# A four-branch mixer trunk on one core: one product drained earlier in the search, a rows unit loaded in halves, and mixer D's tiles solved four at a time

## The chip, the cores and the metric

One core of one Trainium2 chip runs the whole program, in float32. The metric is the device time of one execution in microseconds; the median of three runs is compared.

## The reference, cut to what matters

Two layers run one after the other on x (1024 positions, 1024 channels). Each normalises x, multiplies it by one wide matrix `w_in`, and splits the result into inputs of four mixers, their gates and four merge gates:

```python
for l in range(DEPTH):                                   # 2
    h = _rmsnorm(x, norm_g[l]); p = h @ w_in[l]          # 1024 x 8904
    oa = _chunk_band_attention(aq, ak, av, bias) * silu(az)
    ob = _hgrn2(bq, bf, bi, ...) * silu(bz)              # gated linear recurrence
    oc = _dsa(...) * silu(cz)   # index scores, top 256 keys of each row, attention over them
    od = _rwkv7(dr, dk, dv, wd, ad, ...) * silu(dz)
    y = sum(sigmoid(g_b) * (o_b @ w_branch[l, b]) for b in 'ABCD')
    x = x + y @ w_out[l]
return _rmsnorm(x, final_g)
```

D (`_rwkv7`) is a recurrence over positions with a 64x64 state per head, four heads:

```python
def step(state, xs):
    rt, wt, kt, vt, kkt, at = xs
    sa = einsum('bhvk,bhk->bhv', state, -kkt)
    state = state * wt[:, :, None, :] + sa[..., None] * (kkt * at)[:, :, None, :] + vt[..., None] * kt[:, :, None, :]
    return state, einsum('bhvk,bhk->bhv', state, rt)
```

Its decays and rates come from small products: `tanh(wd) @ w_up` and `ad @ a_up`, each over 64 inner rows.

## The kernel before

Positions stand in eight tiles of 128 (`NT`). The mixers run in the order C, D, B, A; TensorE (`pe`), ScalarE (`act`), VectorE (`dve`), GpSimd (`pool`) and SyncE (`sp`, which issues the loads) each have their own program, written in order, and meet at semaphores.

**Fills.** The projection `h @ w_in` is not a stage of its own. It is cut into steps, and `pe_fill(pe, n)` puts n of them wherever TensorE would otherwise wait; the numbers are the table at the top of the file (`TOPK_FILL`, `D_FILL`, `B_FILL` and others). Blocks of 256 weight columns form units: a column unit has 7 products of four steps (the seven-product form of a 2x2 block product, `PRODUCTS`), and its sums of weight blocks (t1 to t4) and of results are made by GpSimd (`pool_w_sums`, `pool_fills`). A rows unit takes two blocks and computes four pairs of row tiles. Each product goes to one of two PSUM banks (`G`); ScalarE drains it (`act_product`, L528, L537, L541, L547), and `act_fills(act, key)` says up to which point in TensorE's order it drains before it goes on with its own work. Steps of a unit stand at L474 (512 columns) and L471 (256, two matmuls a step). All steps that are left at the end are done before the branch products, so their total does not depend on the tables. `FILL_ORDER` names the projections; gates fill in whenever a projection is not yet free (`next_unit`, `fill_after`).

**The search (C).** After the index scores VectorE looks for the 256th largest score of each row bit by bit, 32 bits (L1481 to L1490); two of the six row tiles are counted by ScalarE with a Sign (L1399). Beside it TensorE does `TOPK_FILL` steps. ScalarE drains between its counts by a formula:

```python
def beside(k, half):
    passed = 10 + (47 * k) // 10 + 2 * half + 7 * sum(k >= bit for bit in qk_bits) + 8 * (k >= 16)
    act_fills(act, ("beside search", min(passed, searched[0] - 1)))
act_fills(act, ("beside search", 12))
```

Then C's attention: scores (L1003), a row maximum on VectorE, Exp on ScalarE (L1083), transposes of the probabilities (L1014) drained by ScalarE (L1069), values (L1027).

**D.** First its products from the two low-rank codes (L1805, 64 rows in the array, eight matmuls through the banks T and O, each drained by a Tanh at L2003), which wait for the tanh of `wd` (L1997). Then norms, bonus and decays, transposes of v (L1831). Then pairs of tiles, four pairs: transposes of keys (L1869), products of keys and queries (L1848, `AG` and `CH`), the values of a chunk (L1856), and five levels that invert a triangular 64x64 system: per level Y (L1856, 16 matmuls of 64x64), masked by VectorE into `yy` (L2147), then X (L1904, 32 matmuls), subtracted by VectorE (L2150, L2151), then the next level. After it the solution (`UZ`), the transitions (`R`, `P`) and four steps of the state, each of which needs the state that VectorE copied (L2172). The table `D_FILL` puts one step after Y, two after X, three at most of the other places. `oD` is the bank of outputs that ScalarE drains (L2037).

**B** begins with its own preparation on VectorE and ScalarE beside `B_FILL["start"]` steps taken four times, then transposes (L1551).

**x.** At the start of layer 0 four DMAs load x, two tiles each (L2272); ScalarE squares and sums each tile (L880), VectorE normalises (L906), TensorE transposes (L413).

## Time and profile before

| what | us |
|---|---|
| median of three runs | 2880.6 (2878.49 to 2882.49) |
| the profiled execution | 2881.09 |
| its span, first to last instruction | 2879.3 |
| TensorE busy, matmuls | 2790.9 (97%), 18640 records |
| VectorE, ScalarE, GpSimd busy | 1584.4, 967.6, 819.7 |
| mean granted TensorE clock | 0.990 |

Times in rows are microseconds from the span's start unless marked ns; PE is TensorE, DVE VectorE, ACT ScalarE, POOL GpSimd. A float32 matmul leaves two records. "[0.59 <-ACT arena L2003]" is idle time of the engine just before a row and what ended it. Merged rows end with the last record's latency, about 0.2 us after the next can begin. PEclk is the granted share of 2.4 GHz: 1.00 is 2.4 GHz, 0.50 is 1.2 GHz. Layer 0 fills 0 to 1440 us, layer 1 the rest, in the same order.

### The profile page before, as it was taken

The page shows a single profiled execution, that of the slowest core. Times are in us where ns is not written, and L with a number is a line of the kernel's source. Part 1 is how long each engine was busy: PE and PEld are TensorE (multiplying, and loading weights), DVE is VectorE, ACT ScalarE, POOL GpSimd, SP SyncE. Part 2 cuts the span into 40 slices and gives each one's busy share as a digit, 9 for nine tenths or more (in the row PEclk, how much of TensorE's full clock was granted, in tenths as well). Part 3 has the DMA queues.
Part 4 walks back from the last instruction along what each step waited for, and adds up shares of the span by engine and source line. Part 5 has one row for each costly group of instructions (what it writes and reads, how often), then busy time and mean ns, then how long its engine had stood idle before and what let it go on. Part 6 is the DMA issues. An engine that isn't in the chain of part 4 may idle for free. (4 is left out here: it accounts for less than half of the span.)

```text
span 2879.3 us, 45819 instructions
## 1 busy us (share of the span) xinstructions
PE 2790.9 (97%) x18640; PEld 1493.9 (52%) x18640; DVE 1584.4 (55%) x2979; ACT 967.6 (34%) x1824; POOL 819.7 (28%) x578
## 2 busy tenths in 40 slices
PE   7999999999999999999999899999999999999998
PEld 4436444477644475444444364544776445654443
DVE  2788865633368813065227888656332787130743
ACT  3345764311143335300114457543111433352001
POOL 4323312321144232233052233123211443212330
PEclk9999999999999999999999999999999999999999
DMA  5212101111121221263042111011011212212731
GB/s 211 63 44 59 45 30 45 44 32 32 35 85 34 96 92 48 99 224 112 0 155 58 51 37 44 30 44 44 32 32 50 70 49 93 77 55 92 239 101 59
DMA packets 134985, 204.61 MB, mean 71 GB/s; under 512 B 8920, under 2 KB 88952, under 8 KB 134008
## 3 DMA queue, kind: packets, MB, share of 16 engines
q1 hardware_dynamic: 116184, 167.59, 18.5%
q10 hardware_dynamic: 18592, 34.09, 3.2%
q8 instruction: 149, 2.44, 0.4%
q14 instruction: 60, 0.49, 0.1%
HBM read 146.07 MB, written 48.78 MB: 68 GB/s over the span
## 5 line engine op out<-in xcount | busy, mean ns | idle before, releaser
L474 PE MATMUL ps<-hT,wr 128*128 128x512 f32 x1792 | 830.7, 601 | 3.6 <-ACT wr L528 2.0
L474 PEld LDWEIGHTS ps<-hT,wr 128*128 128x128 f32 x1792 | 326.7, 191 | 371.0 <-issue 354.7
L474 PE MATMUL ps<-sums,wr 128*128 128x512 f32 x896 | 431.3, 610 | 14.0 <-ACT arena L537 13.9
L634 POOL TENSOR_TENSOR gts<-gts,wr 128x512 f32<-128x512 f32 x96 | 138.0, 1437 | 572.0 <-ACT wr L528 349.4
L474 PEld LDWEIGHTS ps<-sums,wr 128*128 128x128 f32 x896 | 164.2, 194 | 192.8 <-issue 168.4
L1102 DVE CUSTOM_DVE_ANT_0 arena<-ps,arena 128x640 f32<-128x640 f32 (+7 forms) x128 | 90.4, 706 | 306.9 <-PE ps L1003 292.7
L713 PE MATMUL ps<-xo,arena 128*128 128x512 f32 x512 | 220.2, 592 | 1.6 <-ACT gts L541 1.6
L528 ACT ACTIVATE wr<-ps 128x512 f32<-128x512 f32 x168 | 99.6, 593 | 358.6 <-PE ps L474 315.4
L474 PE MATMUL ps<-wr 128*128 128x512 f32 x448 | 210.7, 599 | 1.3 <-ACT wr L528 1.3
L1485 DVE TENSOR_SCALAR_CACHE_REDUCE arena<-arena,sm 128x384 f32<-128x384 uint16 (+7 forms) x256 | 192.8, 809 | 2.2
L607 POOL TENSOR_TENSOR wr<-wr 128x512 f32<-128x512 f32 x62 | 84.7, 1365 | 363.6 <-PE ps L474 356.8
L1399 ACT ACTIVATE arena<-arena,sm 128x896 f32<-128x896 uint16 (+3 forms) x128 | 139.4, 1089 | 69.4 <-DVE sm L1481 69.1
L713 PEld LDWEIGHTS ps<-xo,arena 128*128 128x128 f32 x512 | 97.1, 190 | 124.7 <-issue 124.7
L880 ACT ACTIVATE arena<-arena 128x1024 f32<-128x1024 f32 x24 | 25.4, 1058 | 396.7 <-DVEq L959 392.3
L634 POOL TENSOR_TENSOR arena<-arena,wr 128x512 f32<-128x512 f32 x48 | 79.1, 1649 | 255.8 <-ACT wr L528 173.9
L537 ACT ACTIVATE arena<-ps 128x256 f32<-128x256 f32 (+1 forms) x144 | 68.4, 475 | 214.4 <-PE ps L474 101.7
L471 PE MATMUL ps<-wr,hT 128*128 128x256 f32 x576 | 139.1, 385 | 0.8 <-ACT arena L537 0.8
L1069 ACT ACTIVATE arena<-ps 128x512 f32<-128x512 f32 (+3 forms) x192 | 88.5, 461 | 140.3 <-PE ps L1014 138.7
L547 ACT ACTIVATE gts<-ps 128x512 f32<-128x512 f32 x96 | 57.0, 594 | 220.3 <-PE ps L474 203.4
L474 PEld LDWEIGHTS ps<-wr 128*128 128x128 f32 x448 | 81.1, 190 | 91.3 <-issue 85.8
L1458 DVE SCALAR_TENSOR_TENSOR arena<-arena,sm 128x512 f32<-128x512 f32 (+3 forms) x140 | 104.9, 749 | 28.9 <-ACT arena L1381 24.5
L471 PEld LDWEIGHTS ps<-wr,hT 128*128 128x128 f32 x576 | 106.3, 190 | 18.0 <-ACT arena L537 1.6
(308 smaller groups left out, 4366.8 us busy)
## 6 DMA issues: line engine op xcount, KB each, us to landing
wr<-in_w_in SPq DMA_DIRECT2D x68, 1024.0 KB, 5.3
gate_tanh<-gts ACTq DMA_DIRECT2D x128, 256.0 KB, 2.1
arena<-gate_tanh SPq DMA_DIRECT2D x128, 256.0 KB, 2.9
x_cur<-arena SPq DMA_DIRECT2D x2, 4096.0 KB, 23.0
arena<-in_w_branch SPq DMA_DIRECT2D x8, 1024.0 KB, 9.9
wr<-in_w_out SPq DMA_DIRECT2D x8, 1024.0 KB, 6.6
arena<-x_cur SPq DMA_DIRECT2D x4, 2048.0 KB, 8.8
arena<-arena SPq DMA_DIRECT2D x36, 128.0 KB, 2.8
```

The source lines that it names most:

```text
L471: ins = pe.matmul(ap[:, 0:NCB], lhsT=left(h_side, kt)[:, P * i:P * i + P], rhs=right(u, w_side)[:, kt, :], start=fresh and kt == 0, stop=k ...
L474: ins = pe.matmul(ap, lhsT=right(u, w_side)[:, kt, :], rhs=left(h_side, kt), start=fresh and kt == 0, stop=kt == half_k - 1, skip_group_ch ...
L528: jobs.emptied(act.activation(stage_of(u), src, ACT.Copy), key)
L537: jobs.emptied(act.activation(dest_of[key[:2]](i, slot), src, ACT.Copy), key)
L607: pool.tensor_tensor(t1[:, k0:], b12[:, k0:], b11[:, k0:], ALU.subtract).then_inc(sg("w_sums"), 1)
L634: pool.tensor_tensor(dst, dst, stage_of(u), ALU.add).then_inc(sg("pool_added"), 1)
L713: ins = pe.matmul(ap, lhsT=wbs[ORDER.index(b)][:, k2, P * ct:P * ct + P], rhs=xo[:, 2 * ORDER.index(b) + k2, 512 * half:512 * half + 512], ...
L1069: ins = act.activation(probs_t[u % 3][:, P * g:P * (g + n)], ap[:, 0:P * n], ACT.Copy)
L1102: ins = dve.tensor_tensor_reduce(out=rows[u % 2][:, 0:P * nb], in0=ap[:, 0:P * nb], in1=bias(i, h, nb), scale=HD ** -0.5, scalar=-3e38, op ...
L1399: act.activation(compared[i], half_keys(k // 16, i), ACT.Sign, bias=cand[:, j:j + 1], scale=-1.0, accum_out=count[:, j:j + 1]).then_inc(sg ...
L1458: ins = dve.scalar_tensor_tensor(acc, r, wgt, acc, ALU.mult, ALU.add)
L1485: ins = dve.tensor_scalar(compared[i], half_keys(part, i), cand[:, j:j + 1], None, ALU.is_lt, ALU.add, accum_out=count[:, j:j + 1])
```

## The change

- Search: `TOPK_FILL` 181 becomes 194; ScalarE drains up to step 16 before its first count, and by a new formula beside it. Steps of the key selection are divided differently over four units of attention.
- Rows unit: the second weight block is loaded in two halves (`fill_top_loaded`), the upper one a product earlier; GpSimd makes t1 from the first block and that half, and t2 after it.
- D's first products: `D_FILL["start"]` becomes 4 with 4 more behind a new mark, and ScalarE drains to the mark before the tanh.
- D's tiles by four: two pairs with buffers of their own, level by level in turn, one fill step in each level between Y and X of both; one step of the state of the first pair between solutions of the second. B's projections may begin only when D's outputs are drained, since their place now holds the second pair's buffers.
- Attention: the second transpose group is drained before finished fills, not behind them.
- x: eight loads of one tile.

```diff
-TOPK_FILL = 181
+TOPK_FILL = 194
-D_FILL = {"start": 6, "kk": 23, "bonus": 37, "decay": 11, "nat": 2, "AG": 3, "CH": 3, "Y": 1, "X": 2, "UZ": 3, "P": 3, "S": 1, "norm": 12, "turn": 24}
-B_FILL = {"start": 13, "end": (6, 6), "khn": (3, 2), "adds": (3, 3, 3, 13, 1), "att": 1, "last": 2, "turn": 8}
+D_FILL = {"start": 4, "kk": 23, "bonus": 37, "decay": 11, "nat": (2, 2), "CH": (5, 5), "Y": 1, "UZ": 2, "R": 1, "P": (2, 2), "S": (1, 1), "norm": 13, "turn": 24}
+B_FILL = {"start": 14, "end": (6, 6), "khn": (3, 2), "adds": (3, 3, 3, 13, 1), "att": 1, "last": 2, "turn": 8}
...
-            fill_after = {("B", 0): ("oT", "C", NT - 1), ("B", 3): ("oT", "C", NT - 1), ("B", 1): ("vn", NT - 1),
+            fill_after = {("B", 0): ("oD", NT // 2 - 1), ("B", 3): ("oD", NT // 2 - 1), ("B", 1): ("oD", NT // 2 - 1),
...
+                    if n in second:
+                        top_done = (*done[:3], 4)
+                        loads.append((top_done, wr[:, 2 + n % 2, 0:half_k, 0:w], c0, w, sg("fill_top_loaded"), sums_of, 0))
+                        loads.append((done, wr[:, 2 + n % 2, half_k:, 0:w], c0, w, sg(f"fill_w_loaded{n % 2}"), sums_of, half_k))
+                        continue
...
-                        ap = act_ready(act, ("PT", b, u, g))
+                        key = ("PT", b, u, g)
+                        ap = jobs.ready(act, key) if g else act_ready(act, key)
...
-                        passed = 10 + (47 * k) // 10 + 2 * half + 7 * sum(k >= bit for bit in qk_bits) + 8 * (k >= 16)
+                        passed = 18 + (426 * k) // 100 + 2 * half + sum(n for bit, n in ((4, 9), (12, 9), (16, 9), (23, 3), (27, 2)) if k >= bit)
-                    act_fills(act, ("beside search", 12))
+                    act_fills(act, ("beside search", 16))
...
                     pe_fill(pe, D_FILL["start"])
+                    jobs.mark("before Dw")
+                    pe_fill(pe, 4)
                     pe.wait_ge(sg("wd_tanh"), 1)
...
+                    act_fills(act, "before Dw")
                     act.wait_ge(sg("wd_shifted"), 1)
...
+                    for p in range(0, NT // 2, 2):
+                        turn_keys(p)
+                        pe_fill(pe, D_FILL["nat"][0])
+                        local_products(p)
+                        pe_fill(pe, D_FILL["CH"][0])
+                        turn_keys(p + 1)
+                        chunk_values(p)
+                        pe_fill(pe, D_FILL["nat"][1])
+                        local_products(p + 1)
+                        pe_fill(pe, D_FILL["CH"][1])
+                        chunk_values(p + 1)
+                        for lv in range(1, 6):
+                            for e in range(2):
+                                level_y(p + e, lv)
+                            pe_fill(pe, D_FILL["Y"])
+                            for e in range(2):
+                                level_x(p + e, lv)
+                        for j in range(2):
+                            solve(p, j)
+                        pe_fill(pe, D_FILL["UZ"])
+                        transitions(p)
+                        added_values(p)
+                        pe_fill(pe, D_FILL["P"][0])
+                        state_step(p, 0, 0)
+                        solve(p + 1, 0)
+                        state_step(p, 0, 1)
+                        solve(p + 1, 1)
+                        state_step(p, 1, 0)
+                        pe_fill(pe, D_FILL["S"][0])
+                        state_step(p, 1, 1)
+                        transitions(p + 1)
+                        pe_fill(pe, D_FILL["R"])
+                        added_values(p + 1)
+                        pe_fill(pe, D_FILL["P"][1])
+                        for n in range(4):
+                            if n:
+                                pe_fill(pe, D_FILL["S"][1])
+                            state_step(p + 1, n // 2, n % 2)
...
-                            sp.dma_start(xin[:, 2 * n:2 * n + 2, :], x_pairs[:, 2 * n:2 * n + 2, :]).then_inc(sg(f"x_in{n}"), 16)
+                        for i in range(NT):
+                            sp.dma_start(xin[:, i, :], x_tiles[:, i, :]).then_inc(sg(f"x_in{i}"), 16)
```

Three places of the order, in layer 0. The first is TensorE in D's levels (x counts matmuls, each of which leaves two records in the trace). Before, L1856 is Y and L1904 X, of one pair:

```order
L1856 MATMUL ps<-arena 64x64 x16
L474 MATMUL ps<-hT,wr 128x512
L1904 MATMUL ps<-arena 64x64 x32
L474 MATMUL ps<-hT,wr 128x512 x2
L1856 MATMUL ps<-arena 64x64 x16
L474 MATMUL ps<-hT,wr 128x512
L1904 MATMUL ps<-arena 64x64 x32
```

And in the changed program, where L1873 is Y and L1935 X, of both pairs:

```order
L1873 MATMUL ps<-arena 64x64 x32
L474 MATMUL ps<-hT,wr 128x512
L1935 MATMUL ps<-arena 64x64 x64
L1873 MATMUL ps<-arena 64x64 x32
L474 MATMUL ps<-sums,wr 128x512
L1935 MATMUL ps<-arena 64x64 x64
L1873 MATMUL ps<-arena 64x64 x32
```

The steps after X are gone, and X of the second pair is followed at once by Y of the first pair's next level. The second place is ScalarE at D's first products; before, the tanh of wd (L1997) comes first and the drains of fills behind it:

```order
L1995 ACTIVATE arena<-arena 128x2048
L1997 ACTIVATE arena<-arena 64x1024
L541 ACTIVATE gts<-ps 128x512
L559 ACTIVATE gts<-gts 128x512
L537 ACTIVATE arena<-ps 128x512
L559 ACTIVATE gts<-gts 128x512
L565 DMA gate_tanh<-gts 128x512 x2
L2003 ACTIVATE arena<-ps,sm 128x512 x8
```

Now (L2074 is that tanh, L2080 the drains of D's first products):

```order
L2071 ACTIVATE arena<-arena 128x2048
L547 ACTIVATE gts<-ps 128x512
L2074 ACTIVATE arena<-arena 64x1024
L528 ACTIVATE wr<-ps 128x512
L559 ACTIVATE gts<-gts 128x512
L2080 ACTIVATE arena<-ps,sm 128x512 x8
```

One drain and one tanh are left between the tanh of wd and the drains that TensorE waits for, instead of four operations and two stores. The third place is ScalarE at the search's start, before and now (L1399 and L1411 are the counts, L528 and L537 drains of fills):

```order
L528 ACTIVATE wr<-ps 128x512
L537 ACTIVATE arena<-ps 128x512
L1399 ACTIVATE arena,sm<-arena,sm 128x896
L1399 ACTIVATE arena,sm<-arena,sm 128x1024
L1399 ACTIVATE arena,sm<-arena,sm 128x896
L537 ACTIVATE arena<-ps 128x512
```

```order
L528 ACTIVATE wr<-ps 128x512
L537 ACTIVATE arena<-ps 128x512 x2
L1411 ACTIVATE arena,sm<-arena,sm 128x896
L528 ACTIVATE wr<-ps 128x512
L1411 ACTIVATE arena,sm<-arena,sm 128x1024
L1411 ACTIVATE arena,sm<-arena,sm 128x896
```

A second drain stands ahead of the first count, and the next one between the first two counts instead of behind the third.

## Rows read from the trace of the kernel before

**Rows 1.** The page, part 1: busy time, share, instructions of each engine.

```profile
PE 2790.9 (97%) x18640; PEld 1493.9 (52%) x18640; DVE 1584.4 (55%) x2979; ACT 967.6 (34%) x1824; POOL 819.7 (28%) x578
```

**Rows 2.** TensorE's waits: us in total, times, longest.

```profile
PE ps L474 <- ACT arena L537: 13.9, 2, 7.0
PE ps L413 <- DVE xo L906: 13.8, 1, 13.8
PE ps L1014 <- ACT arena L1069: 10.3, 17, 1.3
...
PE ps L1869 <- issue: 3.4, 6, 0.6
```

**Rows 3.** Timeline, the search's start: start, us, operation; layer 0, last row layer 1.

```profile
199.67 5.63 PE L474 MATMUL ps<-sums,wr 128*128 128x512 f32 x8 [6.97 <-ACT arena L537]
205.13 3.60 PE L474 MATMUL ps<-hT,wr 128*128 128x512 f32 x8
...
194.34 1.04 ACT L1399 ACTIVATE arena<-arena,sm 128x896 f32<-128x896 uint16 x1 [7.88 <-DVE sm L1481]
...
1631.06 6.72 PE L474 MATMUL ps<-sums,wr 128*128 128x512 f32 x8 [6.97 <-ACT arena L537]
```

**Rows 4.** Timeline of TensorE and GpSimd at C's rows unit, layer 0.

```profile
224.00 1.10 PE L471 MATMUL ps<-wr,sums 128*128 128x256 f32 x4 [1.52 <-POOL wr L606]
...
232.25 1.99 PE L471 MATMUL ps<-wr 128*128 128x256 f32 x8 [1.19 <-ACT rows_stage L528]
...
333.38 3.70 PE L474 MATMUL ps<-hT,wr 128*128 128x512 f32 x8 [1.01 <-ACT wr L528]
...
221.23 1.28 POOL L604 TENSOR_TENSOR wr<-wr 128x512 f32<-128x512 f32 x1 [3.10 <-DMA wr<-in_w_in]
```

**Rows 5.** TensorE in a stretch: length, busy (records), PEclk, DMA share, GB/s.

```profile
470.00:480.00 10.00, 10.00 (x13) 0.50 0.00 1
```

**Rows 6.** Timeline of TensorE at D's first products, layers 0 and 1.

```profile
467.22 1.98 PE L1805 MATMUL ps<-arena,par 64*128 64x512 f32 x4 [0.55 <-ACT arena L1997]
469.80 10.04 PE L1805 MATMUL ps<-arena,par 64*128 64x512 f32 x12 [0.59 <-ACT arena L2003]
479.76 5.52 PE L474 MATMUL ps<-hT,wr 128*128 128x512 f32 x8
...
1902.32 9.09 PE L1805 MATMUL ps<-arena,par 64*128 64x512 f32 x12 [0.59 <-ACT arena L2003]
1911.35 4.83 PE L474 MATMUL ps<-hT,wr 128*128 128x512 f32 x8
```

**Rows 7.** Timeline of VectorE as the tiles of x land.

```profile
11.43 0.15 DVE L893 TENSOR_SCALAR sm<-sm 128x1 f32<-128x1 f32 x1 [0.28 <-DMA arena<-in_x]
...
13.97 0.15 DVE L893 TENSOR_SCALAR sm<-sm 128x1 f32<-128x1 f32 x1 [0.28 <-DMA arena<-in_x]
```

**Rows 8.** Timeline of ScalarE in C's attention: a fill's drain.

```profile
407.29 0.58 ACT L528 ACTIVATE wr<-ps 128x512 f32<-128x512 f32 x1
```

**Rows 9.** Timeline of D's levels, layer 0, first pair: TensorE, then VectorE.

```profile
591.49 1.15 PE L1856 MATMUL ps<-arena 64*64 64x64 f32 x32
592.57 1.12 PE L474 MATMUL ps<-hT,wr 128*128 128x512 f32 x2
593.63 1.16 PE L1904 MATMUL ps<-arena 64*64 64x64 f32 x64
...
596.63 1.15 PE L1856 MATMUL ps<-arena 64*64 64x64 f32 x32
...
592.69 0.69 DVE L2147 TENSOR_TENSOR arena<-ps,con 128x512 f32<-128x512 f32 x1 [1.69 <-PE ps L1856]
594.85 0.69 DVE L2150 TENSOR_TENSOR arena<-arena,ps 128x512 f32<-128x512 f32 x1 [1.47 <-PE ps L1904]
595.46 0.68 DVE L2151 TENSOR_TENSOR arena<-arena,ps 128x512 f32<-128x512 f32 x1
```

**Rows 10.** Timeline of TensorE at B's first transposes, layer 0.

```profile
891.40 1.04 PE L1551 MATMUL ps<-con,arena 128*128 128x128 f32 x8
```

More of the change, by code:

```diff
@@ L505, in act_fills @@
                     after = fill_after.get(key[:2])
-                    if after is not None and after[1] == "D":
+                    if after is not None and after[0] == "oT" and after[1] == "D":
                         jobs.stored(act, after)
@@ L1858, in by_chunk, with tiles, turn_keys @@
                         return ins
-                    for p in range(NT // 2):
-                        tiles = ((0, 2 * p), (1, 2 * p + 1))
-                        for j, i in tiles:
+                    def tiles(p):
+                        return ((0, 2 * p), (1, 2 * p + 1))
+                    def turn_keys(p):
+                        e = p % 2
+                        for j, i in tiles(p):
                             t0, t1 = P * i, P * i + P
@@ L1879, in pe @@
-                        jobs.filled(ins, ("CH", p))
-                        pe_fill(pe, D_FILL["CH"])
-                        jobs.stored(pe, ("CH", p))
+                            last = products(ap, i, 0, ((bet, alp, True), (bet, rho, False), (bet, alp, False), (alp, bet, True)))
+                            jobs.filled(last[1], ("AG", i))
+                        for n, bk in enumerate((T, O)):
+                            jobs.open(pe, ("CH", p, n), bk)
+                        for j, i in tiles(p):
+                            last = products(both, i, 2 * j, ((kap, alp, False), (kap, rho, False)))
@@ L1882, in pe, with chunk_values @@
+                        for n in range(2):
+                            jobs.filled(last[n], ("CH", p, n))
+                    def chunk_values(p):
+                        e = p % 2
                         ap = jobs.open(pe, ("CV", p), O)
-                        for j, i in tiles:
-                            ins = by_chunk(ap, 256 * j, HD, ct_[:, j], vn[:, i, :].rearrange("p (h v) -> p h v", h=4))
+                        for j, i in tiles(p):
+                            ins = by_chunk(ap, 256 * j, HD, ct_[e][:, j], vn[:, i, :].rearrange("p (h v) -> p h v", h=4))
@@ new lines, in level_x @@
+                    def level_x(p, lv):
+                        e, key = p % 2, ("X", p, lv)
+                        jobs.stored(pe, ("Y", p, lv))
+                        ap = jobs.open(pe, key, S2[e])
+                        for j in range(2):
+                            for h in range(4):
+                                for crossed, x, y in ((True, xt[e][:, j], yy[e][:, j]), (False, yy[e][:, j], xt[e][:, j])):
+                                    if crossed and lv == 5:
+                                        continue
+                                    for c in range(2):
+                                        rows, c0 = half_rows(c, False), (0 if crossed else 512) + 256 * j + CH * h
+                                        ins = pe.matmul(ap[half_rows(c, crossed), c0:c0 + CH], lhsT=x[rows, h, :], rhs=y[rows, h, :],
+                                                        start=True, stop=True)
+                        jobs.filled(ins, key)
@@ new lines, in solve, with transitions @@
+                    def solve(p, j):
+                        e, i = p % 2, 2 * p + j
+                        pe.wait_ge(sg(f"x_ready{e}"), 6 * (p // 2) + 6)
+                        ap = jobs.open(pe, ("UZ", i), (T, O)[j])
+                        jobs.stored(pe, ("CV", p))
+                        jobs.stored(pe, ("nat", i))
+                        jobs.filled(by_chunk(ap, 0, P, xt[e][:, j], acv[e][:, j]), ("UZ", i))
+                    def transitions(p):
+                        e = p % 2
+                        for j, i in tiles(p):
@@ L1926, in pe, with added_values @@
                                         jobs.filled(ins, ("R", p, c))
+                    def added_values(p):
+                        e = p % 2
                         ap = jobs.open(pe, ("P", p), S2[1])
-                        for j, i in tiles:
+                        for j, i in tiles(p):
                             for h in range(4):
@@ L1952, in pe @@
                                     rows = slice(CH * c, CH * c + CH)
-                                    pe.matmul(o[rows, oc(j, h)], lhsT=gt_[rows, j, h, :], rhs=uz[rows, j, h, HD:], start=j == 0 and h < 2, stop=True,
+                                    pe.matmul(o[rows, oc(j, h)], lhsT=gt_[e][rows, j, h, :], rhs=uz[e][rows, j, h, HD:], start=j == 0 and h < 2, stop=True,
                                               skip_group_check=True)
@@ L2156, in dve, with take_transitions @@
+                        link(dve, ins)
+                        for n in range(2):
+                            jobs.emptied(dve.engine_nop(), ("CH", p, n))
+                        dve.wait_ge(sg(f"x_ready{e}"), 6 * (p // 2) + 1)
+                    def take_transitions(p):
+                        e = p % 2
                         for c in range(2):
```

305 lines of the change are left out of this document (152 added, 153 removed).

## The prediction

> **What bounds the kernel.** I read the busy times of the page first, then TensorE's waits, then the timeline at its longest ones, then the granted clock there. TensorE is busy 2790.9 us of 2879.3, every other engine 55% or less [rows 1]: its own work is the bound. That work is the same after the change: the same products, and 968 fill steps per layer in both programs (a fill step is one float32 128x512 matmul, or two of 128x256; the trace shows each matmul as two records, at 0.4285 us, so a step is 0.857 us). Moving a step costs nothing by itself. The change can only win what lies between: TensorE's idle time, 88.4 us in all, of which four named waits make 41.4 [rows 2]; stretches at the low clock; and the handovers between full-array fills and 64x64 products, which count as busy. What it can lose is new idle time.
>
> **The search.** In both layers TensorE stands 6.97 us, until ScalarE empties a bank. The reader is to see that ScalarE sat 7.88 us at the same time, waiting in order for VectorE's first candidate at 194.34, with a finished product undrained [rows 3]. Behind the gap the clock is granted at the low level, 1.2 GHz: the next eight records take 5.63 and 6.72 us where the same eight take 3.60 at 2.4 GHz. So the price is 2 x 6.97 + 2.03 + 3.12 = 19.1 us. The change drains one more product before that wait (16 steps instead of 12) and one between the first two counts. One product is 3.43 us of TensorE, from 192.6 to 196.0, and the second drain follows ScalarE's count at 194.34 + 1.04, at about 195.4. Gap and low clock both go: **-19.1**. The 13 added steps are 11.1 us of work brought forward, so TensorE reaches the attention when it did before, with VectorE's search ending there too.
>
> **Rows unit.** Here the weight sums come late on GpSimd: it waits 3.10 us for the second weight block, starts at 221.23, and each half sum takes 1.27 [rows 4]. TensorE waits 1.52, then 1.38 for the fourth sum, later 1.19 (stage buffer), 0.42 and 1.01 (drains behind schedule). The upper half of the block now loads one product (3.4 us) earlier and the two halves of t1 need only it, so GpSimd can start when the last product of the unit before ends, at 218.9. t2's first half is then ready about 222.8 against 222.5 wanted, its second 0.3 late; the 1.19 stays near 1.1. Of 4.5 us per layer 2.0 stay: **-5.0** for two layers. The new drain table (4.26 steps per bit, where a bit takes 3.65 us) should remove most of the 1.01 per layer and little else: **-1.3**. Against that, B's three units, which ran among D's products, now run in one piece between D and B (95 steps), so B's rows unit has nothing beside it that hides its first sums and its stage: by the same count 1.5 per layer, **+3.0**. B's own start has 62 steps of fill ahead of its first transpose instead of 58, and TensorE did not wait there [rows 10], so I cost it at nothing; each us by which its chain on VectorE and ScalarE grew past those 3.4 us would be paid in full, twice.
>
> **D's first products.** Two waits, 0.55 (the tanh, ScalarE L1997) and 0.59 (a drain that stands behind ScalarE's other fills), precede sixteen 64-row records [rows 6]. From then on the granted clock is 0.50 [rows 5], and twelve records take 10.04 and 9.09 us against 5.3 at the full clock; the next eight 5.52 and 4.83 against 3.60. Sum: 2.3 + 4.7 + 3.8 + 1.9 + 1.2 = 13.9 us. The change gives two more steps of cover (1.7 us, over the 0.55) and drains older fills before the tanh. What is left is one bank exchange per two matmuls: 0.69 drain plus latencies against the other matmul's 0.857, some 0.1 each, 0.7 in all. What preceded the fall was half-empty rows together with both gaps; with the gaps gone I expect 2.4 GHz to hold: **-13.2**. The low end is -14, the other -2 (clock falls anyway). By the Trainium skill (TensorE: Matmul & The Clock Gate, The HAM clock gate) the gate follows how busy the engine was, idle lowers it and sustained work releases it: by that rule records without gaps keep the high level, and the term would be the same. The trace agrees only in part: twelve 64-row records back to back did not raise it again.
>
> **Loads of x.** Pairs of tiles land 2.54 us apart and VectorE waits for each [rows 7], so a tile is worked off in less than half of that, 1.27, and the second of the last pair only behind the first. Single tiles land 1.27 apart, the last at the same time as now but with nothing ahead of it: VectorE's norm, and with it TensorE's start (the 13.8 in [rows 2]), comes 1.2 us earlier: **-1.2**. Bounds: -2.5 (a whole tile) and +1 (four more issues ahead of the parameters and weights).
>
> **C's attention.** A drain of a finished fill (0.58) stands ahead of the drain of the second transpose group that TensorE waits for [rows 8]; the change turns the two round. It hits perhaps a third of the 17 waits that make 10.3 us. The selection's four steps on VectorE are evened out as well: **-3.0** (0 to -8).
>
> **D's tiles.** In the old levels a period is 5.14 us [rows 9]: 3 steps (2.57), Y's 32 records 0.94, X's 64 records 0.94, so 0.69 goes to four changes of array shape, 0.35 per fill burst. Per two pairs the old program has 36 bursts, the new 17. Outside the levels it is 16 against 12: 4 x 0.35 = 1.4 saved. In the levels 20 bursts become 5, but VectorE now shows. With X0 starting at 0: X0's result reaches VectorE at 1.22, its two subtractions start 0.61 apart and end, with the link, at 2.58; Y0 starts at 2.65, where TensorE was free at 1.88. VectorE turns to X1 at 2.6, is done at 3.96; Y1 starts at 4.02, free at 3.59. Y1 0.94, step and burst 1.21: the next X0 at 6.17. Less its one step that is 5.3; the old two periods less their six steps are 5.14. So 0.17 lost for each of four levels, 0.85 won in the fifth (only one subtraction follows): about nothing, 0.2. Then half of the waits on the output bank at L1869 go (3.4 us in six, [rows 2]): 1.1 per layer, of which I count 0.7. Per layer 2 x (1.4 + 0.2) + 0.7 = 3.9, **-8** for both. Nothing in the old trace shows paired levels; bounds: all 19 bursts won without waits, -27; one more VectorE operation (0.69) exposed in each of the 20 paired levels on top, +6.
>
> New small waits, at the search's end above all: **+1.5**. **Sum:** -19.1 - 5.0 - 1.3 + 3.0 - 13.2 - 1.2 - 3.0 - 8 + 1.5 = -46.3, from the profiled execution's 2881.1 to 2834.8; the median of the runs shown is 0.5 below that execution. I say **2835 us**.
>
> **Rivals.**
> (1) The clock still falls at D's first products, since half the array's rows are empty there with or without gaps. For: the low level held through the twelve back-to-back records. Against: it fell right behind the gaps. 11.5 us are lost: 2846.
> (2) The paired levels wait more than worked out, or run at 1.2 GHz now and then: 0.5 to 1 us in each of 20, so 2845 to 2855. For: between X1 and the next step TensorE does 1.9 us of Y at half the array in some 3.2 us, thinner than anything in the old levels. Against: there the clock is 1.00 throughout, with fills on half the time.
> (3) Slower than before: the low clock through all paired levels. X0, X1, Y0, Y1 and the step double; VectorE's share is hidden under them, and a period is about 9.6 us instead of 6.2. Twenty make +68, total about 2903; it decides from 14 of the 20. Against: at the low clock TensorE would be busy nearly all of that period, and after each low stretch in the trace dense work brought 2.4 GHz back. By the Trainium skill (the same page, A second HAM failure mode: psum-queue depth-cycling) short idles between matmul groups make the gate swing between its levels, which speaks for this one and (2).
> (4) The earlier drains do not carry: VectorE's search ends later than TensorE's 194 steps, and TensorE waits for its first probabilities. ScalarE was held 6 us in the rows unit, and GpSimd's sums then hold it still: some 5 per layer, 2845.
> (5) The paired levels hide better than I think: 2824.
>
> **How the numbers follow.** Forecast 0.50 (own range 2826 to 2844); (1) 0.18, (2) 0.15, (3) 0.03, (4) 0.06, (5) 0.08. The range 2822 to 2856 takes in all but (3) and the tails of (2). No case but (3) comes near 2880; a measurement tells 0.2%, 5.8 us, from no change. Faster by more than that 0.94, within 0.03, slower 0.03.
>
> **What would show it.** No wait on L537 near 193 us and granted clock 1.00 there; L1821's sixteen records (the old L1805) in about 7 us at 1.00; waits on GpSimd's sums under 1 us; new waits of 0.8 and 0.4 on VectorE between X1 and Y1 in each level, and 17 bursts per two pairs; half a wait left at the transposes of keys; attention starting no later. Low clock in 575 to 800 us, or a wait over 2 us at the first probabilities, would prove me wrong.

## The result and the profile after

The changed kernel takes 2854.85 us (median of 4 runs, 2853.26 to 2858.69); the kernel before, beside it, 2881.55 (2878.49 to 2887.02). The ratio is 0.9914, 95% interval 0.9894 to 0.9935. The gain is 26.7 us where 46 was forecast: the sign is right, the size is not. The profiled execution, the slowest of the four, took 2858.69 us, 22.4 less than that of before; the readings below are of these two executions.

The page, part 1, of the changed kernel:

```profile
PE 2770.7 (97%) x18640; PEld 1499.8 (52%) x18640; DVE 1589.2 (56%) x2979; ACT 961.9 (34%) x1820; POOL 844.0 (30%) x578
```

TensorE's waits (us in total, times, longest):

```profile
PE ps L413 <- DVE xo L917: 12.6, 1, 12.6
PE ps L1873 <- DVEq L2276: 10.9, 29, 0.6
PE ps L471 <- POOL wr L608: 8.5, 4, 3.7
PE ps L1025 <- ACT arena L1081: 7.4, 16, 0.8
PE ps L474 <- ACT xo L537: 5.5, 3, 2.2
...
PE ps L471 <- ACT rows_stage L528: 4.2, 5, 1.2
```

Against [rows 1, 2], TensorE is busy 20.2 us less with the same 18640 records, and idle 2.2 us less (86.2 instead of 88.4). The wait of twice 6.97 is gone. In its place stand three groups that the old list did not have at this size: 10.9 us on VectorE in D's paired levels, 8.5 on GpSimd's sum at L608, 5.5 on ScalarE's drain at L537.

To see where the rest went I cut TensorE's timeline at the same operations in both traces and took 0.857 us off for each fill step between two cuts, since steps only move. C's search, for instance, runs from the first index product to the first score product, with 240 steps before and 253 now. The two cuts, before and after:

```profile
90.20 1.77 PE L1358 MATMUL ps<-arena 64*128 64x384 f32 x8
...
350.11 0.49 PE L1003 MATMUL ps<-arena 64*128 64x128 f32 x4
```

```profile
90.20 1.77 PE L1370 MATMUL ps<-arena 64*128 64x384 f32 x8
...
357.74 0.49 PE L1014 MATMUL ps<-arena 64*128 64x128 f32 x4
```

259.9 - 240 x 0.857 = 54.2 us before, 267.5 - 253 x 0.857 = 50.7 now. All stretches, in us against the kernel before (kk is D's product of head sums, vn below stands for the transposes of v ahead of D's first tile):

| stretch of TensorE | forecast, both layers | layer 0 | layer 1 |
|---|---|---|---|
| start to first index product (x) | -1.2 | 0.0 | -0.3 |
| C's search, rows unit, drain table | -25.4, +1.5 small waits | -3.5 | -5.3 |
| C's attention, to its last product | -3.0 | -0.8 | -0.8 |
| D's first products, the wait ahead of them included, to kk | -13.2 | -7.3 | -5.8 |
| kk to D's first tile | 0 | +2.6 | +1.0 |
| D's tiles | -8 | -3.4 | -1.8 |
| D's end to B's first transposes | +3.0 | +2.8 | +2.8 |
| B, A and the output | 0 | -2.5 | -0.1 |
| sum | -46.3 | -12.1 | -10.3 |

Most of the miss is one line: the search wins 8.8 us where 24 was forecast. The first score product stands at 357.74, 7.6 later than before, since the 13 steps brought forward are 11.1 us of work and only 3.5 were won; by the prediction's own sign the attention was to start no later. The -2.5 of layer 0 in the last line is B's attention, from its first transposes to those of its gated outputs: less its steps it takes 35.1 us before and 32.6 now, in layer 1 34.7 and 35.2. Nothing in the forecast orders it, and in b_shift below, which moves 13 steps and nothing else, it takes 33.5 and 32.6, so this part of the gain is luck. The first stall itself is gone. ScalarE at the search's start, changed kernel:

```profile
189.31 0.60 ACT L537 ACTIVATE arena<-ps 128x512 f32<-128x512 f32 x1 [2.84 <-PE ps L474]
194.34 1.04 ACT L1411 ACTIVATE arena<-arena,sm 128x896 f32<-128x896 uint16 x1 [4.43 <-DVE sm L1493]
...
195.38 0.57 ACT L528 ACTIVATE wr<-ps 128x512 f32<-128x512 f32 x1
```

These are the drains at the times forecast, and in 190 to 200 us TensorE is busy throughout at granted clock 1.00, where [rows 3] has the stall. What was won there was lost in two later places. TensorE in the rows unit and at the z gate, then GpSimd and VectorE in the rows unit, and the row of a stretch (length, busy time and records of PE, PEld, DVE, ACT, POOL, granted clock, DMA):

```profile
217.87 4.19 PE L471 MATMUL ps<-wr,sums 128*128 128x256 f32 x8 [3.75 <-POOL wr L608]
221.85 2.67 PE L471 MATMUL ps<-wr,hT 128*128 128x256 f32 x8
...
314.47 7.97 PE L474 MATMUL ps<-hT,wr 128*128 128x512 f32 x14 [2.16 <-ACT xo L537]
```

```profile
211.23 2.08 POOL L604 TENSOR_TENSOR wr<-wr 128x512 f32<-128x512 f32 x1
213.27 2.24 POOL L605 TENSOR_TENSOR wr<-wr 128x512 f32<-128x512 f32 x1
215.48 2.24 POOL L608 TENSOR_TENSOR wr<-wr 128x512 f32<-128x512 f32 x1
...
209.89 2.29 DVE L1449 TENSOR_TENSOR arena<-arena,xo 128x1024 f32<-128x1024 f32 x1
212.22 2.17 DVE L1450 TENSOR_TENSOR arena<-arena 128x1024 f32<-128x1024 f32 x1
214.32 2.28 DVE L1448 TENSOR_TENSOR arena<-arena,xo 128x1024 f32<-128x1024 f32 x1
```

```profile
213.00:220.00 7.00, 3.18 (x11) 1.83 (x9) 6.97 (x4) 0.38 (x1) 7.00 (x5) 0.76 0.00 1
```

GpSimd's sums take 2.1 to 2.2 us each, not 1.28 [rows 4], and VectorE's rotary products beside them 2.2 to 2.3, not 1.2. The third sum ends at 217.72 and TensorE goes on at 217.87. Behind its 3.75 us the clock falls to its low level, 1.2 GHz (0.76 on average in this stretch): eight records take 4.19 us. Without the first stall TensorE reaches the rows unit 8 us earlier (its first product starts at 210.5), on top of VectorE's rotary step of q, which stands at bit 4 of the search. Before, GpSimd started at 221.23, when that step was over.

### The profile page after: what moved, and what is told of

It reads as the page before. It is cut to its first block and busy times, and to the rows that moved or that the text cites. A ratio compares the mean times of both kernels' runs of the same rounds, so it can differ in the third digit from the quotient of the medians.

```text
span 2856.9 us, 45851 instructions
## 1 busy us (share of the span) xinstructions
PE 2770.7 (97%) x18640; PEld 1499.8 (52%) x18640; DVE 1589.2 (56%) x2979; ACT 961.9 (34%) x1820; POOL 844.0 (30%) x578
## 5 line engine op out<-in xcount | busy, mean ns | idle before, releaser
L637 POOL TENSOR_TENSOR gts<-gts,wr 128x512 f32<-128x512 f32 x96 | 159.7, 1663 | 688.4 <-ACT wr L528 422.1
L528 ACT ACTIVATE wr<-ps 128x512 f32<-128x512 f32 x168 | 99.6, 593 | 316.4 <-PE ps L474 272.3
L610 POOL TENSOR_TENSOR wr<-wr 128x512 f32<-128x512 f32 x56 | 79.4, 1417 | 326.9 <-PE ps L474 322.7
L1411 ACT ACTIVATE arena<-arena,sm 128x896 f32<-128x896 uint16 (+3 forms) x128 | 139.4, 1089 | 74.2 <-DVE sm L1493 74.0
L891 ACT ACTIVATE arena<-arena 128x1024 f32<-128x1024 f32 x24 | 25.4, 1059 | 395.5 <-DVEq L970 392.3
L537 ACT ACTIVATE arena<-ps 128x256 f32<-128x256 f32 (+1 forms) x144 | 68.5, 476 | 215.1 <-PE ps L474 123.6
L1081 ACT ACTIVATE arena<-ps 128x512 f32<-128x512 f32 (+3 forms) x192 | 88.4, 461 | 135.3 <-PE ps L1025 133.8
L637 POOL TENSOR_TENSOR arena<-arena,wr 128x512 f32<-128x512 f32 x48 | 67.9, 1415 | 218.2 <-ACT wr L528 126.5
L547 ACT ACTIVATE gts<-ps 128x512 f32<-128x512 f32 x96 | 57.0, 594 | 222.2 <-PE ps L474 218.9
L618 POOL TENSOR_TENSOR wr<-wr 128x512 f32<-128x512 f32 x56 | 87.8, 1568 | 118.7 <-PE ps L474 118.7
## 6 DMA issues: line engine op xcount, KB each, us to landing
x_cur<-arena SPq DMA_DIRECT2D x2, 4096.0 KB, 24.8
```

The costliest lines, as they stand in the source:

```text
L528: jobs.emptied(act.activation(stage_of(u), src, ACT.Copy), key)
L618: pool.tensor_tensor(t4, b21, t2, ALU.subtract).then_inc(sg("w_sums"), 1)
L637: pool.tensor_tensor(dst, dst, stage_of(u), ALU.add).then_inc(sg("pool_added"), 1)
L1081: ins = act.activation(probs_t[u % 3][:, P * g:P * (g + n)], ap[:, 0:P * n], ACT.Copy)
L1411: act.activation(compared[i], half_keys(k // 16, i), ACT.Sign, bias=cand[:, j:j + 1], scale=-1.0, accum_out=count[:, j:j + 1]).then_inc(sg ...
```

## The experiments

All ran against the kernel before, which had medians of 2881.3 to 2881.8 us. The a_ runs are edits of the changed kernel and are set against its 2854.85, the b_ runs edits of the kernel before. Line numbers in rows are each run's own: D's first products are L1805, L1807, L1819 or L1821. "Search" is the stretch of the table, in us of layers 0 and 1: before 54.2 and 55.4, changed 50.7 and 50.1.

**a_rope: VectorE's rotary steps later.**

```diff
-                qk_bits = {4: 0, 12: 1}
+                qk_bits = {9: 0, 14: 1}
-                        passed = 18 + (426 * k) // 100 + 2 * half + sum(n for bit, n in ((4, 9), (12, 9), (16, 9), (23, 3), (27, 2)) if k >= bit)
+                        passed = 18 + (426 * k) // 100 + 2 * half + sum(n for bit, n in ((9, 9), (14, 9), (16, 9), (23, 3), (27, 2)) if k >= bit)
```

> The changed kernel with VectorE's rotary step for q moved from the search's bit 4 to bit 9 and for k from 12 to 14 (the drain table moved with it). Theory A (GpSimd's weight sums of the rows unit now run at the same time as VectorE's rotary products and both are slowed): the sums near 211 us take 1.27 us each instead of 2.06 to 2.24, the three slowed rotary products 1.2 instead of 2.3, TensorE's wait of 3.75 us for the second half of t2 falls below 1 us in both layers and the low clock behind it goes; 6 to 7 us per layer, about 2842 us. Theory B (the sums are late because the weight block's half arrives late or because they start late): the wait stays at 3 us or more, time within 3 us of 2855. Theory C (the search's end on VectorE bounds): the wait goes but TensorE waits as much for the first probabilities, 2850 to 2855.

Measured 2849.27 (2847.84 to 2851.35), ratio 0.9892 (0.9877 to 0.9907); search 46.3 and 46.3. GpSimd and TensorE of this run:

```profile
214.26 1.27 POOL L604 TENSOR_TENSOR wr<-wr 128x512 f32<-128x512 f32 x1
...
216.72 1.27 POOL L608 TENSOR_TENSOR wr<-wr 128x512 f32<-128x512 f32 x1
...
218.13 2.27 PE L471 MATMUL ps<-wr,sums 128*128 128x256 f32 x8 [1.59 <-POOL wr L608]
```

Full-speed sums, full-speed rotary products (1.21 to 1.63), no low clock. The wait is 1.59 rather than under 1, because GpSimd now starts at 214.26, behind an addition. 8.2 us of the stretch come back, 5.6 in the medians, where 12 to 14 was expected; theory A by mechanism, its size too high.

**a_z: one more drain before the z gate.**

```diff
                         if k == Z_BIT:
+                            beside(k, 3)
                             act_z_gate(act)
```

> The changed kernel with one more finished product drained on ScalarE just before the z gate's tanh at bit 22. Theory A (the new drain table leaves a finished product undrained while ScalarE loads its table and does the tanh, 3.1 us): TensorE's waits of 2.16 us near 312 us and in the second layer go, with the low clock behind them, 3 to 4 us per layer, about 2848 us. Rival (ScalarE's drain waits for GpSimd's addition, not for its own order): the waits only move by a product, time within 2 us of 2855.

Measured 2856.24 (2849.06 to 2858.87), ratio 0.9912 (0.9893 to 0.9931): no gain that can be told; search 48.9 and 48.6. The rival is right in its outcome, though not in its reason: the drain waited for ScalarE's own order. The 2.16 is gone, and TensorE waits 2.11 us some 18 us later in both layers, where the changed kernel had 1.21 in layer 1 and nothing over 0.4 in layer 0:

```profile
332.81 2.41 PE L474 MATMUL ps<-sums,wr 128*128 128x512 f32 x5 [2.11 <-ACT xo L537]
```

There ScalarE stands 3.11 us, waiting for bit 27's candidate, while VectorE multiplies in the z gate, with a finished product undrained: the first stall's pattern a third time.

**a_rows_undone: the second block in one piece, sums in the old order.**

```diff
-                    if n in second:
+                    if False:
...
-                        pool.tensor_tensor(t1[:, 0:k0], b12[:, 0:k0], b11[:, 0:k0], ALU.subtract).then_inc(sg("w_half_sums"), 1)
-                        pool.tensor_tensor(t1[:, k0:], b12[:, k0:], b11[:, k0:], ALU.subtract).then_inc(sg("w_sums"), 1)
...
```

> The changed kernel with the rows unit's part undone: the second weight block loads in one piece and both halves of t1 and t2 come in the old order, after the whole block. Theory A (collision with the rotary products is the cost): the sums start near 221 us and take 1.27 us each, the rotary products 1.2; TensorE waits about 1.5 and 1.4 us there instead of 3.75 and 0.53 and the clock stays high; 3 to 5 us per layer gained, about 2847 us. Rival (my forecast for this part: it wins 2.5 us per layer): undoing it costs 5 us, about 2860.

Measured 2861.56 (2858.24 to 2864.88), ratio 0.9934 (0.9918 to 0.995): 6.7 slower than the changed kernel. My expectation was wrong. The sums do not go back to 221 us: they start at 212.61, 1.4 later than with the change, and still meet the rotary step (2.03 to 2.24 us each). TensorE waits 2.80 and 3.22. What sets the moment is when TensorE arrives, not the order of the sums. The size is near the forecast's 5, but most of it comes from another place: C's search is only 0.7 and 1.6 us longer than in the changed kernel (51.5 and 51.7), while the stretch from D's end to B's first transposes is 2.2 longer in both layers. There, in B's rows unit, no rotary step is near, and TensorE waits for two sums instead of 0.48:

```profile
819.39 1.10 PE L471 MATMUL ps<-wr,sums 128*128 128x256 f32 x4 [1.39 <-POOL wr L606]
821.86 1.13 PE L471 MATMUL ps<-wr,sums 128*128 128x256 f32 x4 [1.37 <-POOL wr L611]
```

So this run does not show that the split wins 2.5 us in C's unit of the changed kernel; in B's unit it wins 2.2.

**a_dw_undone: D's first products as before.** In D_FILL "start" is 6 and "kk" 25, and:

```diff
-                    jobs.mark("before Dw")
-                    pe_fill(pe, 4)
-                    act_fills(act, "before Dw")
```

> The changed kernel with the part on D's first products undone: 6 steps ahead of them instead of 4 and 4, no earlier drain (two steps go back behind them). Theory A: two waits of about 0.55 us return, the clock falls to 0.50 in the products and stays there for 20 records, both layers lose what they won, 5 to 6.6 us each: 2865 to 2868 us. Rival (the steps of fill around them or luck set the clock there, not the gaps): the clock stays 1.00 and only about 1 us per layer returns, 2857.

Measured 2858.8 (2856.85 to 2861.5), ratio 0.9926 (0.9908 to 0.9943). The clock stayed at 1.00 and only one wait of 1.07 per layer came back, ahead of a fill. This is 4.0 slower than the changed kernel, near the rival's number; my theory of this part was in doubt, and the next two runs are for it.

```profile
473.48 1.12 PE L474 MATMUL ps<-sums,wr 128*128 128x512 f32 x2 [1.07 <-ACT gts L547]
474.54 7.68 PE L1819 MATMUL ps<-arena,par 64*128 64x512 f32 x16
```

**b_dw: that part alone on the kernel before.** The same edit the other way, with "kk": 21.

> The kernel before with the part on D's first products alone: 4 steps, a mark, 4 steps, and ScalarE drains up to the mark ahead of its tanh (two steps fewer behind). Theory A (the two waits beside the half-empty rows bring the low clock; without them it stays): the sixteen records take 7.7 us in one piece at granted clock 1.00, 5 to 6.6 us per layer gained, about 2869 us. Rival (what decides is at which fills of the unit the products fall, which the search's 13 steps moved, not this part; the run with this part undone kept the high clock): the clock falls to 0.50 here too, 2878 to 2882 us.

Measured 2869.57 (2865.41 to 2872.75), ratio 0.9962 (0.9949 to 0.9975): 11.9 less. The timeline of TensorE, against [rows 6]:

```profile
467.87 7.68 PE L1807 MATMUL ps<-arena,par 64*128 64x512 f32 x16
475.49 1.98 PE L474 MATMUL ps<-hT,wr 128*128 128x512 f32 x4
```

**b_shift: only the place.** The kernel before with `"start": 19` for `"start": 6`, nothing else.

> The kernel before with nothing but 13 more steps of fill ahead of D's first products (19 instead of 6, no mark and no earlier drain), so that these stand at the fill they have in the changed kernel, 13 steps on. The part alone on the kernel before won 12 us, and yet undoing it in the changed kernel cost only its 1 us wait per layer. Theory A (in the changed kernel the products fell at another place in ScalarE's row of fills, where the second wait does not come between the fourth and the fifth record; the place alone keeps the clock): one wait of about 1 us ahead of the sixteen records, these in about 7.7 us at granted clock 1.00, 5 us per layer gained, 2870 to 2872. Rival (the place does not matter and only the extra drain keeps the clock): two waits and 0.50 again, 2879 to 2883.

Measured 2871.16 (2869.47 to 2873.02), ratio 0.9971 (0.996 to 0.9982). One wait of 1.02 ahead of a fill, then sixteen records in 7.68 us at 1.00. So the edit alone keeps the clock, and so does moving the products by 13 steps. Both take away the 0.59 between the fourth and fifth record. The fall comes only with waits on both sides of four half-empty records: in both layers of the kernel before [rows 6], and again in both layers of b_rope7 below (0.55 and 0.59, then twelve records in 9.09 us). No run has one of the two waits without the other at this place, so which of them it takes stays open. The expected 12 us are real, but the search's 13 steps would have brought them anyway.

**a_search_undone: 181 steps, the old drain table.** The 13 steps stand ahead of D's first products ("start" 17).

```diff
-TOPK_FILL = 194
+TOPK_FILL = 181
-                        passed = 18 + (426 * k) // 100 + 2 * half + sum(n for bit, n in ((4, 9), (12, 9), (16, 9), (23, 3), (27, 2)) if k >= bit)
+                        passed = 10 + (47 * k) // 10 + 2 * half + 7 * sum(k >= bit for bit in qk_bits) + 8 * (k >= 16)
-                    act_fills(act, ("beside search", 16))
+                    act_fills(act, ("beside search", 12))
```

> The changed kernel with the search's part undone (181 steps and the old drain table, first drain up to 12; the 13 steps go ahead of D's first products, so that these stay at the same fill). Theory A (the first stall's 7 us were won and given back, since TensorE then reaches the rows unit 8 us earlier, while GpSimd shares time with VectorE's rotary products, and since the new table leaves a product undrained at the z gate): the 6.97 us stall returns, the waits of 3.75 and 2.16 us shrink or go; net loss 3 to 6 us, 2858 to 2861. Rival (my forecast's step: the stall and its low clock are worth 19 us and 1.3 more): 2873 to 2876.

Measured 2860.66 (2857.92 to 2864.12), ratio 0.9934 (0.9912 to 0.9955); search 53.0 and 51.9. This is 5.8 slower than the changed kernel, as theory A has it: with the stall of 6.97 back and its low clock (6.77 for eight records), the search is only 2.3 and 1.8 us longer. The rows unit then meets no rotary step:

```profile
201.26 6.77 PE L474 MATMUL ps<-sums,wr 128*128 128x512 f32 x8 [6.98 <-ACT arena L537]
...
225.74 2.27 PE L471 MATMUL ps<-wr,sums 128*128 128x256 f32 x8 [0.52 <-POOL wr L608]
```

0.52 here against 1.52 and 1.38 in [rows 4] and behind them: 2.4 us per layer, what the forecast gave the rows unit, as long as the stall stands ahead of it.

**b_rope7: the collision made in the kernel before.** One line: `qk_bits = {7: 0, 12: 1}`.

> The opposite test of the collision, on the kernel before: VectorE's rotary step for q moved from bit 4 to bit 7, so that it runs from about 219.7 us, at the same time as GpSimd's sums of the rows unit (221.2 to 229), which it missed. Theory A (each engine stretches the other's tensor-tensor operations over the same memory): sums and rotary products take 2.1 to 2.3 us where they took 1.22 to 1.28; TensorE's waits for the halves of t2, 1.52 and 1.38 us, grow to about 3.4 and 2.3; 3 to 5 us per layer, 2888 to 2892, perhaps a low clock behind them. Rival (the stretch in the changed kernel came from something else of that moment, the weight block landing): sums stay at 1.27, time within 3 us of 2881.

Measured 2891.53 (2890.83 to 2892.56), ratio 1.0035 (1.0022 to 1.0049): 10.3 slower. GpSimd and TensorE of this run:

```profile
222.79 2.12 POOL L606 TENSOR_TENSOR wr<-wr 128x512 f32<-128x512 f32 x1
224.88 2.24 POOL L607 TENSOR_TENSOR wr<-wr 128x512 f32<-128x512 f32 x1
...
225.06 1.10 PE L471 MATMUL ps<-wr,sums 128*128 128x256 f32 x4 [2.25 <-POOL wr L606]
229.38 2.08 PE L471 MATMUL ps<-wr,sums 128*128 128x256 f32 x4 [3.21 <-POOL wr L611]
231.24 3.62 PE L471 MATMUL ps<-wr,hT 128*128 128x256 f32 x8
```

The two waits sum to 5.46 (2.90 before), about half of the 5 us per layer; the other half is the low clock behind them, where eight records take 3.62 instead of 1.89. The first sum starts when the weight block lands, at 221.45 (221.23 before); beside a rotary step the ones behind it stretch in the kernel before as well. This settles the collision.

**a_tiles_undone: D pair by pair, B's units among its fills again.** Its whole D part, D's and B's fills and the places B's fills wait for are those of before; D's first products keep the 4 and 4.

> The changed kernel with D's tiles as before: pair by pair, with the old fills and B's units among them. Forecast for this part: 3.9 us per layer, and B's rows unit then has cover again (1.5 per layer), so undoing costs about 5 us: 2860. Theory A (stage by stage the changed kernel's D wins 1.8 to 3.4 us per layer, B's rows unit loses 2.8 and B's attention wins or loses up to 2.5): undoing costs 2 to 6 us, 2857 to 2861. Rival (the paired levels win much more than the old levels, hidden by waits elsewhere): over 10 us, 2865 or more.

Measured 2860.9 (2858.83 to 2862.28), ratio 0.9935 (0.9912 to 0.9958): 6.0 slower than the changed kernel, as the forecast and theory A have it. D's tiles alone are 3.6 and 2.0 us longer. The stretch up to B's first transposes is no shorter than in the changed kernel.

**a_x_undone: x in pairs of tiles.** The loads and the semaphores they raise are those of before.

> The changed kernel with x loaded in pairs of tiles again. Theory A (TensorE's earlier start is lost at its wait near 52 us, where ScalarE waits for the store of x): first transposes at 13.8 us instead of 12.6, the first index product no later than in the changed kernel, time within 2 us of it (2853 to 2857). Rival (the start is a gain of 1.2 us that is seen only now and then): the index product 1.2 us later.

Measured 2856.32 (2854.31 to 2858.9), ratio 0.9923 (0.9903 to 0.9944): no difference that can be told. The start is 1.3 later, the first index product 0.4. Theory A.

**a_best: the rotary steps and both drains.** a_rope, a_z, and

```diff
-                        if k in qk_bits or k == 16:
+                        if k in qk_bits or k in (16, Z_BIT + 5):
```

> The changed kernel with the rotary steps at bits 9 and 14, one more product drained before the z gate's tanh at bit 22, and one more before ScalarE's long wait for VectorE at bit 27. Theory A (each remaining wait of the search is a finished product that stands undrained behind ScalarE's order): the 2.16 and 1.22 us waits of both layers go; 6 to 7 us under the run with the rotary steps moved alone, 2841 to 2844. Rival (as in the run with the z gate alone, the wait only moves on to the next place): 2847 to 2850.

Measured 2839.34 (2838.57 to 2841.0), ratio 0.9862 (0.9839 to 0.9885), 15.5 less than the changed kernel; search 42.4 and 42.4. The waits of 2.16 and 1.22 that a_rope still has in both layers are gone. Left in its search are:

```profile
216.04 2.27 PE L471 MATMUL ps<-wr,sums 128*128 128x256 f32 x8 [1.60 <-POOL wr L608]
...
222.98 1.99 PE L471 MATMUL ps<-wr 128*128 128x256 f32 x8 [1.21 <-ACT rows_stage L528]
```

**a_best2: fills among the bonus products.** a_best with "kk" 22 and

```diff
-                    pe_fill(pe, D_FILL["bonus"])
+                    pe_fill(pe, D_FILL["bonus"] - 3)
...
                     for i in range(NT):
+                        if i in (2, 4, 6):
+                            pe_fill(pe, 1)
...
-                        pe_fill(pe, D_FILL["decay"])
+                        pe_fill(pe, D_FILL["decay"] + (n == 2))
```

> The run a_best with three of the fill steps put among the 32 two-column bonus products, which alone take 3.63 us, and one step moved from ahead of kk to behind the decay. Theory A (behind these thin products the clock is granted at 0.50 in most runs, 1.6 to 4.2 us per layer; with fills between them it stays, and the 0.79 wait at the vn transposes goes): 4 to 7 us below a_best, 2833 to 2836. Rival (the low clock comes from the thinness even so, or moves to the next place): 2838 to 2841.

Measured 2836.94 (2833.79 to 2839.22), ratio 0.9855 (0.9835 to 0.9875), the lowest median here; 2.4 less than a_best is under what can be told. In the profiled executions the stretch from the bonus products to the vn transposes falls from 6.3 to 4.6 us in both layers, and the low clock there is gone; the 0.79 wait stayed. That the edit did it is not shown: a_tiles_undone has 4.6 in both layers too, with the 32 bonus products in one piece of 3.63 us and granted clock 1.00 behind them, and one layer each of a_rows_undone and a_x_undone has 4.6 as well.

## Why the prediction was off

**The search, -19.1, and the rows unit, -5.0: the failed steps.** Of the 23.9 us that the profiled executions lack, 15.1 are here. The stall goes as worked out. The working then took the rows unit's prices as if they did not depend on when it runs: "each half sum takes 1.27", start at 218.9, waits under 1 us. In the changed kernel the sums start at 211.23, share time with the rotary step and take 2.1 to 2.2. TensorE waits 3.75 in each layer, and the low clock behind it costs 2.7 in the first (4.19 + 2.67 against a_search_undone's 2.27 + 1.89) and 3.2 in the second (4.19 + 3.20). a_rope, b_rope7 and a_search_undone show this step from both sides. I had named the 8 us shift only for the end of the search, not for what TensorE would meet on the way. The trace of before held a warning that I read past. GpSimd's addition and VectorE's rotary step met there for one operation, and it took 2.29 beside five of 1.22 to 1.23 (the addition, at 212.87, took 1.78):

```profile
212.31 1.22 DVE L1436 TENSOR_TENSOR arena<-arena,xo 128x1024 f32<-128x1024 f32 x1
213.44 2.29 DVE L1437 TENSOR_TENSOR arena<-arena,xo 128x1024 f32<-128x1024 f32 x1
```

By the Trainium skill (SBUF — State Buffer, Who interferes with whom) a VectorE instruction with two inputs in SBUF and a GpSimd instruction that reads SBUF exclude each other: whichever starts first keeps the shared port to its end. The trace agrees: 2.24 is a sum's own 1.27 and about 1 us more, which is what is left of the other engine's operation if the two alternate, and beside VectorE's counting instructions, which have one such input, sums take 1.27. Read beside [rows 3, 4], this would have given the collision as a rival with its price.

**The drain table, -1.3.** It removed the 1.01 and put 2.16 at the z gate of both layers and 1.21 at bit 27 of layer 1 in its place, with a low clock behind the 2.16 of layer 0 (14 records in 7.97 us; 14 x 0.4285 is 6.0). At the z gate ScalarE loads a table (1.28) and does a tanh (1.91) ahead of the drain. The rule that found the first stall (a finished product stands undrained while ScalarE waits or works in order) holds at both places; I had not followed the new table that far. Moving the rotary steps gives 8.2 us of the search back (a_rope) and the two drains 7.8 more (a_best). With all three put right, a_best's search is 11.8 and 13.0 us shorter than before, 24.8 in all, against 25.4 forecast for the three terms. So a gain of this size was there to be had, and the change gave two thirds of it back; but a_best has three edits that the change lacks, so that the two sums are close confirms no single term.

**D's first products, -13.2**, came as -13.1, with the clock held as forecast, and b_dw gives 11.9 for the edit alone. That this edit is what brings it here was too narrow: b_shift and a_dw_undone show that the shift of 13 steps does it too.

**Loads of x, -1.2.** TensorE starts 1.2 earlier and waits 1.25 at 53.10 us instead of 0.30, on ScalarE, which waits 14.29 for the store of x. The next thing late was not named:

```profile
52.45 1.08 ACT L661 ACTIVATE arena<-ps 128x512 f32<-128x512 f32 x2 [14.29 <-DMA x_cur<-arena]
...
53.10 3.27 PE L474 MATMUL ps<-hT,wr 128*128 128x512 f32 x7 [1.25 <-ACT arena L661]
```

**C's attention, -3.0**, came as -1.6. The waits for the drains of its transposes fell from 10.3 to 7.4 us in the list, but the stretch is only 0.8 shorter in each layer; no run isolates the two edits made there.

**D's tiles, -8**, came as -5.2. The level was right: all sixteen periods are 6.11 us (worked out 6.17), with waits of 0.55 and 0.18 that the rows count from the end of the last record's latency, some 0.2 late, so 0.75 and 0.38 where 0.77 and 0.43 were worked out, and no low clock in 575 to 800 us, so rivals (2) and (3) fell:

```profile
606.69 1.15 PE L1873 MATMUL ps<-arena 64*64 64x64 f32 x32 [0.55 <-DVEq L2276]
608.02 1.15 PE L1873 MATMUL ps<-arena 64*64 64x64 f32 x32 [0.18 <-DVEq L2276]
609.10 1.13 PE L474 MATMUL ps<-hT,wr 128*128 128x512 f32 x2
610.16 2.10 PE L1935 MATMUL ps<-arena 64*64 64x64 f32 x128
612.80 1.15 PE L1873 MATMUL ps<-arena 64*64 64x64 f32 x32 [0.55 <-DVEq L2276]
```

The 2.8 is missing outside the levels, where the two layers differ too (-3.4 and -1.8 for the whole); no run splits it further.

**B's rows unit, +3.0**, cost 5.6 up to B's first transposes. Per layer TensorE waits 0.48 on the sums and 1.21 on the stage buffer, and eight records behind the first take 2.27 where the next eight take 1.89, 0.38 more; the last 0.7 I can't place. The count from C's rows unit (1.5) left out the stage wait's full size. a_tiles_undone is 5.5 longer than the kernel before in the same stretch too, but there from two waits on drains (0.75 and 1.46), so that run doesn't test this term.

```profile
819.57 2.27 PE L471 MATMUL ps<-wr,sums 128*128 128x256 f32 x8 [0.48 <-POOL wr L608]
821.67 1.89 PE L471 MATMUL ps<-wr,hT 128*128 128x256 f32 x8
...
826.49 1.99 PE L471 MATMUL ps<-wr 128*128 128x256 f32 x8 [1.21 <-ACT rows_stage L528]
```

**Not in the sum:** behind the 32 bonus products TensorE ran longer at the low clock, +2.6 and +1.0 up to D's first tile. From the bonus to the vn transposes the runs have anything between 3.7 us (b_dw) and 7.9, and no edit here is shown to order it.

Of the rivals, (4) came nearest in one remark (GpSimd's sums hold ScalarE around the rows unit, some 5 per layer); it had 0.06. Its mechanism did not happen: it put the loss at the search's end, and there the attention starts without a wait. No rival named the collision.

## What to carry to other kernels

A stall that is taken away moves everything behind it: go through what the bottleneck engine will meet that much earlier, and ask of each engine that feeds it what it shares its time with at the new moment. A price read in one row ("1.27 each") holds for that row's neighbours only; an outlier of the same operation in the old trace tells what the price is beside others. And when the same pattern (a finished product undrained behind an in-order wait) explains one stall, follow the new order to its end for the next place.

## What was not expected of the hardware

GpSimd's 128x512 sums take 1.27 us alone, 2.0 to 2.2 beside VectorE's tensor-tensor operations on SBUF, and these go from 1.22 to 2.3; brought about in the kernel before (b_rope7), it costs 5 us per layer, half of it wait and half low clock. Sixteen half-empty 64-row records keep the 2.4 GHz level in 7.68 us when they run in one piece, even 1 us behind a wait of about 1 us; with waits of 0.55 and 0.59 around the first four the clock fell to 1.2 GHz in both layers of the kernel before and of b_rope7.
